# Gated attention started two weight units sooner, its steps spread over more units, two heads to a PSUM bank, convolution ahead of the output gate

## What is computed

```python
def hybrid_mixer(h, w_in, sc_conv_w, sc_conv_b, gla_w_gate, gla_b_gate, gla_norm_g, w_out, slopes):
    proj = h @ w_in
    (c_b, c_c, c_h, m_q, m_k, m_v, g_q, g_k, g_v, g_o, g_lr) = jnp.split(proj, points, axis=-1)
    y_conv = c_b * causal_dwconv(c_c * c_h, sc_conv_w, sc_conv_b)
    y_moba = moba_attention(hs(m_q, N_MOBA_HEADS), hs(m_k, N_MOBA_HEADS), hs(m_v, N_MOBA_HEADS), slopes)
    log_a = jax.nn.log_sigmoid((g_lr @ gla_w_gate + gla_b_gate).astype(jnp.float32)) / GLA_GATE_NORMALIZER
    o = gla_attention(hs(g_q, N_GLA_HEADS), hs(g_k, N_GLA_HEADS), hs(g_v, N_GLA_HEADS), hs(log_a, N_GLA_HEADS))
    y_gla = rmsnorm_2(o, gla_norm_g).reshape(Bsz, T, GLA_WIDTH) * jax.nn.silu(g_o)
    return jnp.concatenate([y_conv, y_moba, y_gla], axis=-1) @ w_out
```

## The kernel before

| unit | PE | ACT | DVE |
|---|---|---|---|
| 3 | gate logits (semaphore g_p 1) | Abs, Exp, Ln (L1526 to L1530) | min, subtract, scale |
| 4 | running sum (g_p 2) | copy b, exponentials, decay (L1533 to L1540) | |
| 5 | | | q exp(b), k exp(-b), kend (L2197 to L2199) |
| 6 | scores of heads 0 to 3 (g_p 3 to 6), in banks 6 and 7 in turn; heads 2 and 3 wait for ACT's copies of heads 0 and 1; then kend transposed (g_p 7, L1059) after the copy of head 3 | four copies (L1545), copy of the transposed kend (L1547) | |
| 7 | chunk states 0, 1, 2 (g_p 8 to 10); state 2 waits until DVE took state 0 out of bank 7 | | masks and recurrence (L2206, L2210) |
| 8 | outputs (g_p 11, 12) | copies (L1552) | |
| 9 | mean square (g_p 13), after ACT's Square | Square (L1555) | |
| 10 | | reciprocal root (L1558) | |
| 11 | | | refinement of the root (L2219, L2221, L2223) |
| 12 | | high half of the result (L1562), needs L2229 | gain (L2226), output gate (L2229) |
| end | | | low half of the result (L2232) |

## Time and profile before

### The profile page before, as it was taken

How to read it: one execution, slowest core, us unless ns; L and a number is a source line. 1 busy time by engine, 2 the same in 40 slices (tenths; PEclk the granted TensorE clock), 3 DMA queues, 4 the chain that set the end, 5 groups by cost and what they waited for, 6 DMA issues and landing times.

```text
span 1531.4 us, 25416 instructions
## 1 busy us (share of the span) xinstructions
PE 1451.4 (95%) x10172; PEld 1348.2 (88%) x10172; DVE 1075.0 (70%) x1888; ACT 862.4 (56%) x1475; POOL 433.4 (28%) x257
## 2 busy tenths in 40 slices
PE   4999999899999999999999999999989989799997
PEld 3988978899999999999988888888878879699997
DVE  7678868566779788888656666677644546587853
ACT  4444664544455788888645444555444644666651
POOL 2222100234345312212123322343263213233210
PEclk9999999999999999999999999999999999899999
DMA  9747746455555544444456666656675324276540
GB/s 362 244 137 256 244 162 220 162 169 165 185 176 174 169 139 144 144 139 140 146 171 220 193 194 192 220 179 192 196 274 167 108 70 152 70 235 184 188 124 28
DMA packets 74007, 269.26 MB, mean 176 GB/s; under 512 B 8433, under 2 KB 9762, under 8 KB 73122
## 3 DMA queue, kind: packets, MB, share of 16 engines
q1 hardware_dynamic: 71568, 257.46, 52.6%
q10 hardware_dynamic: 1426, 7.56, 1.3%
q0 software_dynamic: 896, 2.62, 0.5%
HBM read 263.93 MB, written 3.67 MB: 175 GB/s over the span
## 4 chain that ended last, share of the span: by engine, by line
PE 82%; DVE 7%; ACT 5%; issue 2%; POOL 2%; DMA 1%; SPq 0%; ACTq 0%; DVEq 0%; POOLq 0%
PE bank L557 82%; DVE split L1641 2%; ACT split L1152 2%; POOL split L2333 1%; DVE ada_acc L1678 1%; DMA xT<-in_xT 1%; DMA far<-in_w_ada 1%; ACT PB L1259 0%; POOL PB L2347 0%; PE bank L721 0%; DVE sm L1765 0%; ACT PA L1259 0%; DVE H L2131 0%; DVE rT L1719 0%; DVE xT L1733 0%
## 5 line engine op out<-in xcount | busy, mean ns | idle before, releaser
L557 PE MATMUL bank<-H,split 128*128 128x256 f32 x6120 | 773.5, 287 | 22.1 <-DVE split L1641 7.5
L557 PEld LDWEIGHTS bank<-H,split 128*128 128x128 f32 x6120 | 751.6, 194 | 30.1 <-issue 14.7
L1152 ACT CAST split<-ringb 128x1024 fp32r<-128x1024 f32 x350 | 367.3, 1050 | 281.3 <-PE bank L557 273.8
L2333 POOL TENSOR_TENSOR split<-ringb,split 128x1024 fp32r<-128x1024 f32 x115 | 286.9, 2496 | 628.7 <-ACT split L1152 628.7
L557 PE MATMUL bank<-split,H 128*128 128x512 f32 (+1 forms) x1728 | 391.4, 388 | 4.6 <-DVE H L2131 1.8
L557 PEld LDWEIGHTS bank<-split,H 128*128 128x128 f32 x1728 | 321.8, 189 | 72.2 <-issue 3.9
L1641 DVE TENSOR_TENSOR split<-ringb,split 128x1024 fp32r<-128x1024 f32 x235 | 295.7, 1260 | 91.8 <-ACT split L1152 91.7
L2131 DVE TENSOR_TENSOR H<-PR,H 128x256 fp32r<-128x256 f32 x128 | 134.3, 1051 | 107.5 <-ACT H L1468 107.3
L1641 DVE TENSOR_TENSOR split<-far,split 128x1024 fp32r<-128x1024 f32 x75 | 103.9, 1391 | 61.6 <-ACT split L1152 61.6
L1152 ACT CAST split<-far 128x1024 fp32r<-128x1024 f32 x91 | 94.9, 1049 | 70.3 <-PE bank L557 64.8
L2094 DVE TENSOR_SCALAR xT<-cst,rt 128x128 f32<-128x128 f32 x168 | 87.2, 582 | 0.0
(11 more groups left out here) (271 smaller groups left out, 1269.0 us busy)
## 6 DMA issues: line engine op xcount, KB each, us to landing
ringb<-in_u SPq DMA_DIRECT2D x128, 512.0 KB, 3.7
ringb<-in_v SPq DMA_DIRECT2D x128, 512.0 KB, 4.4
ringb<-in_w_ada SPq DMA_DIRECT2D x28, 512.0 KB, 5.2
far<-in_w_up SPq DMA_DIRECT2D x27, 512.0 KB, 4.4
far<-in_w_ada SPq DMA_DIRECT2D x20, 512.0 KB, 5.3
ringb<-in_w_up SPq DMA_DIRECT2D x17, 512.0 KB, 4.3
ringb<-in_w_pq SPq DMA_DIRECT2D x16, 512.0 KB, 4.0
far<-in_w_dn SPq DMA_DIRECT2D x14, 512.0 KB, 3.6
```

The costliest lines, as they stand in the source:

```text
L557: return TE.matmul(o, l, r, start=start, stop=stop, skip_group_check=True)
L1152: S.copy(buf(m)[0], slots[P.slot[m]]).then_inc(hi_done, 1)
L2333: G.tensor_tensor(lo, slots[P.slot[m]], hi.bitcast(F32), ALU.subtract).then_inc(lo_g, 1)
```

## The change

- `gla_steps` is started on PE, ACT and DVE at unit 1, ahead of `w2_gk`, instead of unit 3 (POOL's start stays, its first step is one unit later).
- Yields are added, so that the steps lie at these units: PE gate logits 1, running sum 3, scores 6, transposed kend 7, states 8, outputs 10, mean square 11. ACT: Abs/Exp/Ln 1, exponentials 3, copies of scores 6, copy of kend 7, output copies and Square 10, reciprocal root 11, high half in `finish`. DVE: log gate 1, q/k products 4, states 8, refinement of the root 11, gain and output gate 12, low half in `finish`.
- The scores of heads 0 and 2 share bank 6 and those of 1 and 3 bank 7, in different columns. Heads 2 and 3 wait for PE's own semaphore (heads 0 and 1 written) and not for ACT. ACT copies in two instructions of 128x512 instead of four of 128x256.
- The states 0 and 2 lie in different columns of bank 7, so that none waits for DVE.
- The units after `w2_gv` come in the order `w2_cc` (5, 6), `w2_ch` (7, 8), `w2_cb` (9, 10), `w2_go` (11, 12), in the stream of DMAs, in the bank assignment and in all programs. Their number is unchanged, and so is which unit POOL takes.
- On DVE the convolution's taps become a job of two steps beside `w2_cb`; the product with `w2_cb` follows unit 10, its low half lies between units 11 and 12, and `lows_ahead` comes after unit 12's step. On ACT the high half of the convolution (waits for DVE's product) comes before the cast of unit 11's turn, and Silu after unit 12.

```diff
...
     P.add("w2_xv", 2, "four")
-    for nm, k in [("w2_mq", 4), ("w2_mk", 4), ("w2_mv", 4), ("w2_lr", 1), ("w2_gk", 2), ("w2_gv", 2), ("w2_go", 2),
-      ("w2_cc", 2), ("w2_ch", 2), ("w2_cb", 2), ("w2_o", 8), ("w2_xk", 2), ("w2_xq", 2), ("w2_xo", 2), ("w_up", 44), ("w_dn", 22)]:
+    for nm, k in [("w2_mq", 4), ("w2_mk", 4), ("w2_mv", 4), ("w2_lr", 1), ("w2_gk", 2), ("w2_gv", 2),
+      ("w2_cc", 2), ("w2_ch", 2), ("w2_cb", 2), ("w2_go", 2), ("w2_o", 8), ("w2_xk", 2), ("w2_xq", 2), ("w2_xo", 2), ("w_up", 44), ("w_dn", 22)]:
         P.add(nm, k, "far2")
...
         + [("lin", "w2_mq", 4, 8), ("lin", "w2_mk", 4, 8), ("nat", "w2_mv", 512), ("one", "w2_lr"), ("lin", "w2_gk", 2, 8),
-           ("nat", "w2_gv", 256), ("lin", "w2_go", 2, 8), ("lin", "w2_cc", 2, 8), ("lin", "w2_ch", 2, 8), ("lin", "w2_cb", 2, 8),
+           ("nat", "w2_gv", 256), ("lin", "w2_cc", 2, 8), ("lin", "w2_ch", 2, 8), ("lin", "w2_cb", 2, 8), ("lin", "w2_go", 2, 8),
            ("lin", "w2_o", 8, 8), ("lin", "w2_xk", 2, 8), ("lin", "w2_xq", 2, 8), ("lin", "w2_xo", 8, 2), ("lin", "w_up", 44, 8), ("lin", "w_dn", 8, 22)])
...
         ("w2_mq", 2, "A", 1), ("w2_mk", 2, "A", 1), ("w2_mv", 2, "A", 1), ("w2_lr", 1, "A", 1), ("w2_gk", 1, "A", 1), ("w2_gv", 2, "A", 1),
-        ("w2_go", 1, "A", 1), ("w2_cc", 1, "A", 1), ("w2_ch", 1, "V", 1), ("w2_cb", 1, "V", 1), ("w2_o", 4, "V", 2), ("w2_xk", 1, "A", 1), ("w2_xq", 1, "A", 1),
+        ("w2_cc", 1, "A", 1), ("w2_ch", 1, "V", 1), ("w2_cb", 1, "V", 1), ("w2_go", 1, "A", 1), ("w2_o", 4, "V", 2), ("w2_xk", 1, "A", 1), ("w2_xq", 1, "A", 1),
         ("w2_xo", 4, "V", 2), ("w_dn", 4, "V", 2)]
...
 
-GA = dict(bT=4, dec=11, at=11, ke=16, o=16, sq=19)
+GA = dict(bT=4, dec=11, at=11, ke=14, o=14, sq=17, rt=18, hi=19)
 GV = dict(min=1, la=3, qk=6, S=7, ms=13, lo=17)
...
 one("w2_lr", hk, mh)
-lin("w2_gk", 2, hk, mh)
 
...
     yield
+    yield
     o = claim(7)
...
     yield
+    yield
+
...
         if h >= 2:
-            t.wait_ge(g_a, GA["at"] + h - 1)
-        b = 6 + h % 2
+            t.wait_ge(g_p, h + 1)
         for tt in range(2):
-            last = mm(banks[b][:, tt * 128:(tt + 1) * 128], en[32 * h:32 * h + 32, tt * 128:(tt + 1) * 128],
+            c = 256 * (h // 2) + tt * 128
+            last = mm(banks[6 + h % 2][:, c:c + 128], en[32 * h:32 * h + 32, tt * 128:(tt + 1) * 128],
                       eb[32 * h:32 * h + 32, tt * 128:(tt + 1) * 128], True, True)
         last.then_inc(g_p, 1)
-    t.wait_ge(g_a, GA["at"] + 3)
+    yield
+    t.wait_ge(g_a, GA["at"] + 1)
     for tt in range(2):
...
         r = slice(64 * (c % 2), 64 * (c % 2) + 64)
-        if c == 2:
-            t.wait_ge(g_v, GV["S"])
-        mm(banks[7 - c % 2][:, 0:256], keN[r, (c // 2) * 128:(c // 2) * 128 + 128], gv[r, (c // 2) * 256:(c // 2) * 256 + 256],
+        o = banks[6][:, 0:256] if c == 1 else banks[7][:, 128 * c:128 * c + 256]
+        mm(o, keN[r, (c // 2) * 128:(c // 2) * 128 + 128], gv[r, (c // 2) * 256:(c // 2) * 256 + 256],
            True, True).then_inc(g_p, 1)
+    yield
     yield
...
 jobs.start(gla_steps())
+lin("w2_gk", 2, hk, mh)
 lin_nat("w2_gv", hkt, mh, 256)
-lin("w2_go", 2, hk, mh)
 lin("w2_cc", 2, hk, mh)
...
 lin("w2_cb", 2, hk, mh)
+lin("w2_go", 2, hk, mh)
 jobs.finish()
...
 copy_out("w2_lr", 0, lrT[0:16, :], T, 16)
-lin_copy("w2_gk", 2, gqk)
 
...
     eb, en, kend, keN = gt[:, 512:768], gt[:, 768:1024], gt[:, 1024:1280], gt[:, 1792:2048]
-    AT = sc_g[:, 0:1024].rearrange("p (h t c) -> p h t c", h=4, t=2)
     oF = gt[:, 2048:2560]
...
     yield
+    yield
     s.wait_ge(g_p, 2)
...
     yield
-    for h in range(4):
-        s.wait_ge(g_p, 3 + h)
-        S.copy(AT[:, h, :, :], banks[6 + h % 2][:, 0:256].rearrange("p (t c) -> p t c", t=2)).then_inc(g_a, 1)
+    yield
+    for i in range(2):
+        s.wait_ge(g_p, 5 + i)
+        S.copy(tri3(sc_g[:, 0:1024], 4)[:, i:4:2, :], tri3(banks[6 + i][:, :], 2)).then_inc(g_a, 1)
+    yield
     s.wait_ge(g_p, 7)
     S.copy(keN, banks[6][:, 0:256]).then_inc(g_a, 1)
+    yield
     yield
...
         S.copy(oT[:, pr, :], banks[6 + pr][:, 0:256]).then_inc(g_a, 1)
-    yield
     s.wait_ge(g_a, GA["o"] + 2)
...
 jobs.start(gla_steps())
+lin_copy("w2_gk", 2, gqk)
 nat_copy("w2_gv", gv, 256)
-units("w2_go", 2)
-S.activation(goT, take_out("w2_go", 0), ACT.Silu).then_inc(ev_a, 1)
 lin_copy("w2_cc", 2, ccT)
...
 S.copy(flat(Ym[:, 0, 0:2, :]), ctmp).then_inc(cv_hi, 1)
+units("w2_go", 2)
+S.activation(goT, take_out("w2_go", 0), ACT.Silu).then_inc(ev_a, 1)
 jobs.finish()
...
 unit("w2_lr")
-units("w2_gk", 2)
 
...
     yield
+    yield
     v.wait_ge(g_a, GA["dec"])
...
     yield
+    yield
+    yield
     for c in range(3):
-        v.wait_ge(g_p, 8 + c)
+        v.wait_ge(g_p, 10)
         if c == 0:
             v.wait_ge(gc_in, 16)
-        V.tensor_tensor(St[:, c, :].rearrange("p (h e) -> p h e", h=4),
-                        banks[7 - c % 2][:, 0:256].rearrange("p (h e) -> p h e", h=4), hm2, ALU.mult).then_inc(g_v, 1)
+        o = banks[6][:, 0:256] if c == 1 else banks[7][:, 128 * c:128 * c + 256]
+        V.tensor_tensor(St[:, c, :].rearrange("p (h e) -> p h e", h=4), o.rearrange("p (h e) -> p h e", h=4),
+                        hm2, ALU.mult).then_inc(g_v, 1)
         if c:
...
     t_, rr = sc_g[:, 1024:1536], sc_g[:, 0:512]
-    yield
-    v.wait_ge(g_a, 20)
+    v.wait_ge(g_a, GA["rt"])
     V.tensor_tensor(t_, sqg, sqg, ALU.mult).then_inc(g_v, 1)
...
     yield
-    v.wait_ge(g_a, 21)
+    v.wait_ge(g_a, GA["hi"])
     V.tensor_tensor(flat(Ym[:, 1, 6:8, :]), oF, flat(Ym[:, 0, 6:8, :]).bitcast(F32), ALU.subtract).then_inc(g_v, 1)
...
 jobs.start(gla_steps())
+units("w2_gk", 2)
 units("w2_gv", 2)
-units("w2_go", 2)
 units("w2_cc", 2)
...
 V.tensor_tensor(uv[:, :, 2:258], tri3(o[:, :], 2), tri3(ccT, 2), ALU.mult).then_inc(ev_v, 1)
+cc = Tally(cv_c)
+
+def conv_steps():
+    v.wait_ge(*evac("w2_ch", 0))
+    v.wait_ge(cv_z, 1)
+    for j in range(2):
+        c_ = ctmp[:, j * 256:(j + 1) * 256]
+        cc.up(V.tensor_scalar(c_, uv[:, j, 2:258], vec("sc_w", 4 + j), vec("sc_b", j), ALU.mult, ALU.add))
+        for tap in (1, 0):
+            v.wait_ge(cc.sem, cc.n)
+            cc.up(V.scalar_tensor_tensor(out=c_, in0=uv[:, j, tap:tap + 256], scalar=vec("sc_w", 2 * tap + j), in1=c_,
+                                         op0=ALU.mult, op1=ALU.add))
+        yield
+
+jobs.start(conv_steps())
 units("w2_cb", 2)
-cc = Tally(cv_c)
-v.wait_ge(*evac("w2_ch", 0))
-v.wait_ge(cv_z, 1)
-for j in range(2):
-    c_ = ctmp[:, j * 256:(j + 1) * 256]
-    cc.up(V.tensor_scalar(c_, uv[:, j, 2:258], vec("sc_w", 4 + j), vec("sc_b", j), ALU.mult, ALU.add))
-    for tap in (1, 0):
-        v.wait_ge(cc.sem, cc.n)
-        cc.up(V.scalar_tensor_tensor(out=c_, in0=uv[:, j, tap:tap + 256], scalar=vec("sc_w", 2 * tap + j), in1=c_,
-                                     op0=ALU.mult, op1=ALU.add))
-lows_ahead()
 v.wait_ge(cc.sem, cc.n)
...
 V.tensor_tensor(ctmp, o[:, :], ctmp, ALU.mult).then_inc(ev_v, 1)
+unit("w2_go")
 v.wait_ge(cv_hi, 1)
 V.tensor_tensor(flat(Ym[:, 1, 0:2, :]), ctmp, flat(Ym[:, 0, 0:2, :]).bitcast(F32), ALU.subtract).then_inc(cv_lo, 1)
+unit("w2_go")
+lows_ahead()
 jobs.finish()
...
     yield
+    yield
     for h in range(4):
-        g.wait_ge(g_a, GA["at"] + h + 1)
+        g.wait_ge(g_a, GA["at"] + h % 2 + 1)
         G.affine_select(out=AT[:, h, :, :], in_=AT[:, h, :, :], compare_op=ALU.is_ge, fill=0.0, base=0,
...
 jobs.start(gla_steps())
-units(sum(P.part[n] for n in ("w2_gv", "w2_go", "w2_cc", "w2_ch", "w2_cb")))
+units(sum(P.part[n] for n in ("w2_gv", "w2_cc", "w2_ch", "w2_cb", "w2_go")))
 jobs.finish()
...
```

## The result

The changed kernel takes 1525.68 us (median of 15 runs) against 1532.08 us for the kernel before (15 runs), so the medians are 6.4 us apart. The ratio that the comparison of the runs gives is 0.9948, with an interval of 0.9936 to 0.9959: 8.0 us less, 6.3 to 9.8. One of the 15 executions of the changed kernel took 6441.89 us and is left out of the ratio as slow; why it was is not known, and the other 14 lie between 1520.9 and 1528.84 us. The profiled execution took 1525.87 us, with a span of 1524.1 us.

A forecast was written before the change was run, and what follows sets the result against it. PE, busy 95% of the span, was taken as the bound, so only its idle or slow time could be gained. 8.1 us gained less 1.1 in the tail gave 7.0: median 1530.46 to 1523.5 us, 8-in-10 range 1519.8 to 1527.6.

The forecast's parts named there:

- Units 6, 7 and 9: PE's waits of 1.67, 0.19, 2.57 and 1.18 us in these units would go.
- rival of a partial effect: A moved step meets a wait hidden behind the old ones: gain only about 3 us, 1527.5 us; chance 0.10.
- self-wait of the scores: Unit 6: heads 2 and 3 wait for PE's own heads 0 and 1, costing 0.3 us, bounds 0 to 0.4.
- The clock: Low clock at units 6 and 7 goes: 2.3 us in the units, 0.5 in small matmuls, together 2.8 us.
- rival that the low clock stays: Idle time goes but PE stays at low clock: gain 4.2 us, 1526.3 us; chance 0.10.
- Gate logits at unit 1: Starting the gate at unit 1 makes PE wait nowhere, and ACT's lateness is covered: cost nothing.
- slower rival: Gate work on ACT at unit 1 delays the attention, PE waits at each transposition: 1535.5 us; chance 0.05.
- Order of units, DMAs, POOL: Same number of matmuls, casts, low halves and DMAs, POOL keeps its units: nothing gained or lost.
- The tail: Wait ahead of `w2_o` grows from 3.70 to 4.8 us behind ACT's root and DVE's queue: 1.1 us given back.
- T: The end of unit 10's matmuls on PE, from which the tail is timed; `w2_o` was forecast at T + 11.3.
- The table load: Rival: a drain beside the tail's load makes the root 1.4 us later: gain 5.6, 1524.9 us; chance 0.03.
- The clock of `w2_o`: Low clock at the start of `w2_o` loses the same 2.7 us as before, 1.3 us either way.

The follow-up runs named there:

- fill experiment: The changed kernel with 34 more matmuls, whose result nothing reads, between unit 12 and `w2_o`: `w2_o` takes 22.68 us, ratio to the kernel before 0.9942.
- banks only: The kernel before with two heads of scores to a bank, two copies, states in their own columns: 69.68 us from unit 0 to `w2_o`, ratio 0.9959.
- new order only: The kernel before with only the new order of units and of the convolution: 74.61 us from unit 0 to `w2_o`, ratio 0.9980.
- unit 13's low half sooner: The changed kernel with DVE making unit 13's low half right after the convolution's, ahead of the root's refinement: ratio to the kernel before 0.9911.

## Why the prediction was right, point by point

**Units 6, 7 and 9.** The four waits, 5.61 us in all, are gone as forecast, and nothing took their place. The rival of a partial effect falls.

**The self-wait of the scores.** Sized at 0.3 us between 0 and 0.4. It is 0: the row of 24 small matmuls at 1218.15 has no idle bracket. That head 1, issued between head 0 and head 2, covers it is likely but was not tried. The chosen row (a turn to another engine and back) was the wrong neighbour.

**The clock.** The term that was mis-sized most up to unit 12. 9.14 us went up to the end of unit 12, of which 5.61 was idle; 3.5 remain for the clock, against 2.8 forecast. The two units alone are the 2.3 us that were read from the earlier trace rows, so by difference the small matmuls beside them lost 1.2 us and not 0.5 (inside the bound of 1.4). The trace of before agrees: PEclk is 0.71 from 1219.65 to 1225.50 us and 0.68 from 1230.70 to 1236.00, which is 3.4 us at 1.2 GHz each, and half of that, 1.7 us each, is lost against full clock. The fill experiment shows the same mechanism by itself. The rival that the low clock stays falls: PEclk is 1.00.

**Gate logits at unit 1.** No idle bracket before them, and none at any transposition: the early gate does not make the attention late enough to matter. The slower rival is not seen.

**Order of units, DMAs, POOL.** Nothing, as forecast.

**The tail.** Forecast: a wait of 4.8 us made by ACT's root at T + 4.5 and 6.8 us of DVE's queue behind it. T is 1245.26 (1242.15 and 3.11 us of matmuls), and the rows are, on ACT:

```profile
1246.09 0.62 ACT L1576 CAST Ym<-PB 128x512 fp32r<-128x512 f32 x1 [2.68 <-DVE PB L2268]
1246.62 1.04 ACT L1156 CAST split<-far 128x1024 fp32r<-128x1024 f32 x1
1247.68 1.28 ACT L1563 ACT_TABLE_LOAD   x1
1248.97 0.69 ACT L1563 ACTIVATE PB<-bank,sm 128x512 f32<-128x512 f32 x1
1249.56 1.04 ACT L1156 CAST split<-ringb 128x1024 fp32r<-128x1024 f32 x1
1250.62 1.28 ACT L1578 ACT_TABLE_LOAD   x1
1251.91 0.60 ACT L1578 ACTIVATE PB<-bank 128x512 f32<-128x512 f32 x1
```

and on DVE:

```profile
1249.76 0.69 DVE L2227 TENSOR_TENSOR sc_g<-PB 128x512 f32<-128x512 f32 x1 [3.71 <-ACT PB L1563]
...
1251.21 0.69 DVE L2231 SCALAR_TENSOR_TENSOR sc_g<-sc_g,PB 128x512 f32<-128x512 f32 x1
1251.94 0.69 DVE L2271 TENSOR_TENSOR Ym<-PB,Ym 128x512 fp32r<-128x512 f32 x1
1252.55 1.22 DVE L1647 TENSOR_TENSOR split<-far,split 128x1024 fp32r<-128x1024 f32 x1
1253.68 0.75 DVE L2234 SCALAR_TENSOR_TENSOR PB<-PB,vecs,sc_g 128x512 f32<-128x512 f32 x1
1254.46 0.69 DVE L2237 TENSOR_TENSOR PB<-PB 128x512 f32<-128x512 f32 x1
1255.07 1.22 DVE L1647 TENSOR_TENSOR split<-ringb,split 128x1024 fp32r<-128x1024 f32 x1
```

The root is there at 1249.66, T + 4.4. DVE starts at 1249.76, and PE at 1256.39: 6.6 us. The order on the queue is the one worked out, to the last instruction, and the low half of unit 14 ends it. Silu was ready at 1252.51 and asked for at 1254.46. The wait is 4.52 us; the term was 0.3 too large: DVE's queue and the root came 0.2 us sooner than the sum of their rows, since rows overlap by a few hundredths each, and PE's two units ended at T + 6.6 and not T + 6.5. That this queue is the cause is shown by the two kernels that only change its order.

**The table load.** Load at 1247.68, activation at 1248.97; Silu's load at 1250.62, right behind a cast that began at 1249.56 and takes 1.04. There is no room for a drain of 1.4 us behind or ahead of a load, so that rival falls. The Trainium skill (ScalarE: Activation LUTs, section What ACT_TABLE_LOAD costs) has 1.28 us for the load, which agrees, and a drain of 1.38 us beside it, which these rows don't show; the measurement decides.

**The clock of `w2_o`.** Taken as equal, it was 1.0 us better, inside its bounds; of all terms this one was furthest off. In the first 10 us of `w2_o` PEclk is 0.72 before and 0.83 after, that is 5.6 and 3.4 us at 1.2 GHz; half of the difference, 1.1 us, accounts for the 1.0 us. Before, the low clock was there already when `w2_o` started at 1262.78, and lasted into this window, more than 5 us later:

```profile
1268.00:1269.00 1.00, 1.00 (x9) 1.00 (x8) 0.00 (x0) 0.00 (x0) 0.00 (x0) 0.79 0.86 303
```

The length of the wait does not decide it: banks only has the wait of before (3.69 us) and takes 24.22 us, as after does with 4.52 us and new order only with 2.67. All nine other traces are better than the single one of before. A longer and a shorter low stretch are also seen at 200 to 210 us, in code that no variant changes (PEclk 0.66 and 0.83). So this 1.0 us is more likely chance of that one execution than a gain of the change, but it is not shown.

**The sum.** Forecast 7.0 us. The stretch gave 9.3 (8.3 to `w2_o`, 1.0 in it), the comparison of many runs 8.0, with 6.3 to 9.8. The 2.3 us between forecast and stretch are 0.3 of the self-wait, 0.7 of the clock up to unit 12, 0.3 of the tail and 1.0 of the clock of `w2_o`, all to the same side. The forecast's span of 1524.4 against 1524.1 looks better than it was, and that is luck: 2.3 us more gain in the stretch and an arrival at unit 0 that was 1.9 us later nearly cancelled. The forecast median of 1523.5 us was 2.2 us under the measured 1525.68, which lies just above its narrower bounds (1521.5 to 1525.5) and inside the range of 8 in 10. Most of that is the starting point: the forecast was added to the 1530.46 us of three runs, and the 15 runs of the kernel before had 1532.08. The medians themselves moved by 6.4 us, against 7.0 forecast.

## What to carry to other kernels

A wait of TensorE costs its length and then the slow matmuls behind it; here the clock's share was more than half as much again, and all small matmuls around the wait belong in it. Ask first whether a bank has room for the next result: giving each result its own columns, with half as many copies, took four fifths of this gain up to `w2_o` without moving a step. Here a reader was started only when both results in its bank were written. When a tail is given a longer queue, write that queue out instruction by instruction: what PE waits for should not stand at its end, and the best version here came from moving two low halves ahead of work that nobody needed yet. Last, take single profiles apart by stretch and by PEclk: two executions of the same instructions differed here by more than most of the variants.

## What the runs showed of the hardware

- From unit 0 to the end of `w2_o`, the granted clock fell to 1.2 GHz during or after waits of 1.67, 2.23, 2.57, 2.67, 3.69, 3.70, 4.52 and 5.38 us, and not after 0.42, 0.44, 0.51, 0.75, 1.07, 1.18 and 1.40 us. How long it stayed down was not fixed: around waits of 3.70 and 3.69 us, with the same instructions, PEclk in the first 10 us of `w2_o` was 0.72 and 0.83, and `w2_o` took 25.22 and 24.22 us.
- At full clock throughout (PEclk 1.00), the 192 matmuls of `w2_o` still took 21.85 us with unit 13's low half sooner and 22.68 with PE kept busy. What sets this was not tried.
- The first projection of the program started between 38.96 and 42.61 us in kernels with the same instructions ahead of it, and unit 0 between 1183.0 and 1190.8 us. With the same instructions from 200 to 210 us, PEclk was 0.66 or 0.67 in five traces and 0.83 in five, and the first five took 1146.6 to 1148.2 us from the first projection to unit 0, the others 1144.0 to 1145.3. This spread is larger than most effects studied here, so single profiled spans should not be compared before it is taken off.
